# DIFF's sub-norm root by bits, exp and Newton steps on GpSimd; later transposes; compressed transposes in the other PSUM bank

## Chip, cores, metric

One core of a Trainium2 chip. The metric is the device time of one launch in microseconds. The engines are TensorE (PE; its weight loads are PEld), VectorE (DVE), ScalarE (ACT), GpSimd (POOL) and SyncE (SP), which issues all DMAs here. Each runs its own instructions in program order; they meet at semaphores.

## The reference, cut to what matters

The program is one layer of a decoder on 512 tokens of width 1024 in fp32: a combined projection, three token mixers (NSA: compressed, selected and window attention; DIFF: differential attention; FOX: forgetting attention), gates that merge them, an output product and a convolutional feed-forward part. The change lies in DIFF's sub-norm and in the start of NSA's compressed attention. The sub-norm:

```
ob = diff_attention(qb, kb, dv.reshape(B, S, DIFF_HEADS, 2 * hd), lam)
o_b = (rms_norm(ob, diff_subln_g[l]) * (1.0 - lam_init)).reshape(B, S, BRANCH_WIDTH)
# rms_norm(x, g) = x * rsqrt(mean(x * x) + EPS) * g, over the 128 values of each head
```

So each of the 512 tokens and 4 heads needs one value (mean + EPS) ** -0.5: four columns of 128 rows for each block of 128 tokens.

## The kernel before, in words

Every fp32 product is made of fp32r pieces: a weight block comes by DMA into `raw`, ScalarE rounds it to `wh`, VectorE subtracts to get `wl`, and TensorE runs three passes (L1277 to L1279). There are three attention stages in a row: NSA, DIFF, FOX. Each is laid out as a list of events in slots by `attention_events` (`put(j, ...)`), and all engines walk the same list, each doing its part of every event and waiting on semaphores for the others.

In DIFF there are 32 score units (4 query blocks of 8: 4 heads by 2 maps); the keys grow from 128 to 512 with the block. The events of a slot come in this order: S (TensorE's scores L1425 to L1428 in one of two banks; VectorE's maximum L1048; ScalarE's Exp L737, which frees the bank), C (VectorE's combination of two maps, L1053 to L1058, at every even slot), G (about five of the 192 gate products, L1455; after every 24th ScalarE takes a Tanh, L753), A (transposes of the combined probabilities, L1305, copied by VectorE L1067 or ScalarE L743), O (values, L1441; copied by VectorE into `otok`, L1077), SUB, SUN, OT, WL (VectorE's weight piece, L850), W (ScalarE's, L585). A unit's values come five slots behind its scores, so the last of block i falls in slot 8(i + 1) - 1 + 5, called `last`: 12, 20, 28, 36.

The sub-norm of block i: SUB at `last`: ScalarE squares `otok` (L768) and loads the table set that has Ln and Exp (L769), VectorE sums per head into `hss` (L1108). SUN one slot later: ScalarE takes Ln (L594) and Exp with scale -0.5 (L595) in `inv_rms`, VectorE multiplies `otok` by the result (L1112). OT three slots after `last` (the last block: between the two halves P of FOX's query projection): TensorE transposes `otok` (L1305), ScalarE rounds with the gain into `oT_h` (L777), VectorE takes the rest into `oT_l` (L1116). `otok` has two buffers, by the block's parity.

Behind the last slot the list goes on with the weight pieces W and WL of the projection's second half, then P 0, OT, P 1; then `post` takes the norms of FOX's queries, again with `inv_rms`. GpSimd copies keys before DIFF's slots (L1247, L1248), and merges branch results after them (L1255); between these it has no work.

In NSA's head the order is written out by hand (`first`): gate products G, and SC (compressed scores), CN (their softmax), T (transposes of window keys), TC (transposes of the compressed probabilities, copied by ScalarE to `pcT`, L762), OC (their values). SC, TC and OC use the bank that the running gate chunk of 24 products does not use: `spare = 1 - f // GATE_STEPS % 2`.

Of the kernel before, what the change touches and what calls it, by code (L numbers as in the profile page):

```python
# [19 lines left out]

P = 128
S = 512
# [2 lines left out]
TT = S // P  # L25
# [82 lines left out]
def attention_events(m):  # L108

    U = len(units_of(m))
    per = U // TT
    t_lag, o_lag = (3, 5) if m == DIFF else (2, 3)
    at = {}  # L120

    def put(j, *event):
        at.setdefault(j, []).append(event)

    tail = 20 if m == FOX else 0
    head = HEAD_FILL[m]
    slots = U + o_lag
    for piece in range(4):
        if m > NSA:
            put(piece, "W", BI[(m, "gate1")], piece)  # L130
            put(piece + 1, "WL", BI[(m, "gate1")], piece)

    def put_fill(j, f0, f1):
        put(j, "G", f0, f1)
        for f in range(f0, f1):
            if (f + 1) % (2 * GATE_STEPS) == 0:
                b = BI[(m, "gate0")] + f // (2 * GATE_STEPS) + 2
                for piece in range(4):

                    if m < FOX or b < BI[(m, "gate3")] + 2:  # L140
                        put(j + 1 + piece, "W", b, piece)
                        put(j + 2 + piece, "WL", b, piece)

    if m == NSA:

        head = 40
        for i in range(1, TT):
            put(per * i - 12, "SC", i)
            put(per * i - 10, "CN", i)
            put(per * i - 8, "TC", i)  # L150
            put(per * i - 6, "OC", i)
    for j in range(slots):
        n = FILL - tail - head
        put_fill(j, head + n * j // slots, head + n * (j + 1) // slots)
        if j < U:
            put(j, "S", j)
    for q in range(U):
        if has_pv(m, q):
            put(q + 1, "C", q)
            put(q + t_lag, "A", q)  # L160
            put(q + o_lag, "O", q)
    for i in range(TT):
        last = per * (i + 1) - 1 + o_lag
        if m == DIFF:
            put(last, "SUB", i)
            put(last + 1, "SUN", i)
            if i < TT - 1:
                put(last + 3, "OT", i)
        elif i < TT - 1:
            put(last + 1, "OT", i)  # L170
    order = {k: n for n, k in enumerate(("S", "C", "CN", "TC", "OC", "G", "SC", "A", "O", "SUB", "SUN", "OT", "WL", "W"))}
    out = [e for j in sorted(at) for e in sorted(at[j], key=lambda e: order[e[0]])]
    first = [("G", 0, HEAD_FILL[m])]
    if m == NSA:
        b = BI[(m, "gate1")]
        first = [("G", 0, 8), ("SC", 0), ("W", b, 0), ("G", 8, 16), ("CN", 0), ("WL", b, 0), ("W", b, 1), ("G", 16, 24), ("T", 0), ("WL", b, 1),
                 ("W", b, 2), ("TC", 0), ("G", 24, 32), ("T", 1), ("WL", b, 2), ("W", b, 3), ("OC", 0), ("WL", b, 3), ("G", 32, head)]
    if m == FOX:
        out += [("G", FILL - tail, FILL - 8), ("OT", TT - 1), ("G", FILL - 8, FILL), ("W", BI[(m, "gate3")] + 2, None), ("WL", BI[(m, "gate3")] + 2, None)]
    else:  # L180
        out += [("P", 0), ("OT", TT - 1), ("P", 1)]
    return first + out


def build(nc, x, wblk, w1, w2, params, consts, out):
# [85 lines left out]
    with ExitStack() as ctx:  # L271
# [113 lines left out]
        neglam = small("neglam", [P, 1])  # L385
        valid = small("valid", [P, 1])
        kss = small("kss", [HD, 1])
        assert base + used[0] <= nc.sbuf_usable_end, (base + used[0], nc.sbuf_usable_end)

        ps = [ctx.enter_context(nc.psum_tensor(f"ps{i}", [P, S], f32)) for i in range(8)]  # L390

        def sem(name):
            return ctx.enter_context(nc.semaphore(name))
# [29 lines left out]
        const_ready = sem("const_ready")  # L423
        k_zero = sem("k_zero")
        k_twice = sem("k_twice")
        cpe_ready = sem("cpe_ready")
        ksq_ready, kss_ready = sem("ksq_ready"), sem("kss_ready")
        sub_sq = sem("sub_sq")
# [68 lines left out]
        NORMS = [n for m, n in NORM_JOBS]  # L497

        rs_order = [("N", 0), ("nq", 0), ("nq", 1), ("KC",)] + [(n, r) for n in ("sw", "dq", "dk") for r in range(2)]
        rs_order += [("SUB", i) for i in range(TT)] + [(n, r) for n in ("fq", "fk") for r in range(2)] + [("N", 1)]  # L500
        rs_at = {k: n + TT for n, k in enumerate(rs_order)}

        def operands(m, u):
# [62 lines left out]
        def _(act):  # L566
# [128 lines left out]
            for m in (NSA, DIFF, FOX):  # L695
# [33 lines left out]
                for e in EVENTS[m]:  # L729
                    what, j = e[0], e[1] if len(e) > 1 else None  # L730
                    if what == "T":
                        post_t(m, PROJ[m][-1], (2 * j, 2 * j + 1))
                    if what == "S":
                        s0, n = span(units[j])
                        b = place[("S", m, j)][0]
                        act.wait_ge(max_ready, unit_no(m, j) + 1)
                        nc.scalar.activation(prob[:, j % 4, 0:n], ps[b][:, 0:n], ACT.Exp, bias=nmx[:, j:j + 1],  # L737
                                             accum_out=lsum[:, j:j + 1]).then_inc(psum_free[b], 1)
                    elif what == "A" and pv_index(m, j) % 2 == 1:
                        s0, n = span(units[j])  # L740
                        b = place[("A", m, j)][0]
                        full(act, ("A", m, j))
                        nc.scalar.activation(probT[:, 1, 0:n], ps[b][:, 0:n], ACT.Copy).then_inc(psum_free[b], 1)  # L743
                    elif what == "G":
                        for f in range(e[1], e[2]):
                            if (f + 1) % GATE_STEPS == 0:
                                c = f // GATE_STEPS
                                full(act, ("G", m, c))
                                if m > NSA:
                                    free(act, ("B", m - 1, c))  # L750
                                b = place[("G", m, c)][0]

                                nc.scalar.activation(gate[:, c, :], ps[b][:, :], ACT.Tanh, scale=0.5).then_inc(psum_free[b], 1)  # L753
                    elif what == "W":
                        split(j, e[2])
                    elif what == "SC":
                        free(act, ("SC", j))
                        nc.scalar.activation(pc[:, j % 2], pc[:, j % 2], ACT.Exp).then_inc(cexp_ready, 1)
                    elif what == "TC":
                        b = place[("TC", j)][0]  # L760
                        full(act, ("TC", j))
                        nc.scalar.activation(pcT[:, :, :], ps[b][:, 0:256].rearrange("p (e t) -> p e t", e=2),  # L762
                                             ACT.Copy).then_inc(psum_free[b], 1)
                    elif what == "SUB":
                        last = len(units) // TT * (j + 1) - 1
                        free(act, ("O", m, last - 2))
                        free(act, ("O", m, last))
                        nc.scalar.activation(sq[:, 0, :], otok[:, j % 2, :], ACT.Square).then_inc(sub_sq, 1)  # L768
                        nc.scalar.preload_act_table_set(LN_EXP)  # L769
                    elif what == "SUN":  # L770
                        act.wait_ge(sub_sums, j + 1)
                        inv_rms(rstd[:, 4 * j:4 * j + 4], hss[:, j, 0:4], P)
                    elif what == "OT":
                        b = place[("OT", m, j)][0]
                        full(act, ("OT", m, j))

                        nc.scalar.activation(oT_h[:, :, j * P:(j + 1) * P], ps[b][:, :].rearrange("p (k t) -> p k t", k=4), ACT.Copy,  # L777
                                             scale=par[:, C_SUBLN:C_SUBLN + 1] if m == DIFF else 1.0).then_inc(oT_hi, 1)
# [56 lines left out]
        def _(dve):  # L835
# [174 lines left out]
            for m in (NSA, DIFF, FOX):  # L1010
# [28 lines left out]
                for e in EVENTS[m]:  # L1039
# [67 lines left out]
                        dve.wait_ge(sub_sq, j + 1)  # L1107
                        nc.vector.tensor_reduce(hss[:, j, 0:4], sq[:, 0, :].rearrange("p (h c) -> p h c", c=P), AX.X, ALU.add).then_inc(sub_sums, 1)  # L1108
                    elif what == "SUN":
                        dve.wait_ge(rstd_ready, rs_at[("SUB", j)])  # L1110
                        v = otok[:, j % 2, :].rearrange("p (h c) -> p h c", c=P)
                        nc.vector.tensor_tensor(v, v, rstd[:, 4 * j:4 * j + 4].unsqueeze(2).to_broadcast([P, 4, P]), ALU.mult).then_inc(sub_ready, 1)  # L1112
                    elif what == "OT":
                        dve.wait_ge(oT_hi, TT * m + j + 1)
                        b = place[("OT", m, j)][0]
# [102 lines left out]
        @block.gpsimd  # L1218
        def _(pool):

            pool.wait_ge(const_in, 32)
            full(pool, ("N", 0, KD - 1))
            nc.gpsimd.tensor_copy(valid[:, :], stage[:, K_VALID:K_VALID + 1])
# [19 lines left out]
            for m in (DIFF, FOX):  # L1243
                for c in range(4):

                    pool.wait_ge(hi_taken, hi_at[("T", m, PROJ[m][1], c)])
                    nc.gpsimd.tensor_copy(k_hh[64:128, 2 * c, :], k_hh[0:64, 2 * c, :])  # L1247
                    nc.gpsimd.tensor_copy(k_hh[0:64, 2 * c + 1, :], k_hh[64:128, 2 * c + 1, :]).then_inc(k_twice, 1)  # L1248
                for c in range(KD):

                    free(pool, ("B", m, c))
# [475 lines left out]
```

## Time and profile before

| | us |
|---|---|
| median of 3 runs | 1028.97 |
| lowest, highest | 1026.33, 1029.14 |
| profiled execution, its time | 1028.74 |
| profiled execution, its span | 1027.0 |
| busy PE, DVE, ACT, POOL | 1004.2, 561.5, 402.1, 95.9 |

The profile is of one execution. Its span leaves out 1.7 us that the time has around it. Times in rows count from the span's start. DIFF's slots run from about 324 to 411 us; the NSA head from about 88 to 104 us. TensorE counts as busy while a product runs, also at half clock, so its busy time alone does not tell whether it runs at full speed; the granted clock (1.00 for 2.4 GHz, 0.50 for 1.2 GHz, a mean over a window) does.

### The profile page before, as it was taken

The page shows a single profiled execution, that of the slowest core. Times are in us where ns is not written, and L with a number is a line of the kernel's source. Part 1 is how long each engine was busy: PE and PEld are TensorE (multiplying, and loading weights), DVE is VectorE, ACT ScalarE, POOL GpSimd, SP SyncE. Part 2 cuts the span into 40 slices and gives each one's busy share as a digit, 9 for nine tenths or more (in the row PEclk, how much of TensorE's full clock was granted, in tenths as well). Part 3 has the DMA queues.
Part 4 walks back from the last instruction along what each step waited for, and adds up shares of the span by engine and source line. Part 5 has one row for each costly group of instructions (what it writes and reads, how often), then busy time and mean ns, then how long its engine had stood idle before and what let it go on. Part 6 is the DMA issues. An engine that isn't in the chain of part 4 may idle for free.

```text
span 1027.0 us, 13047 instructions
## 1 busy us (share of the span) xinstructions
PE 1004.2 (98%) x5101; PEld 844.2 (82%) x5101; DVE 561.5 (55%) x1035; ACT 402.1 (39%) x729; POOL 95.9 (9%) x84
## 2 busy tenths in 40 slices
PE   6999999999999899999999999999999999999998
PEld 5777889998888677888888888888888888888887
DVE  5746887763565576456555445465655565621213
ACT  5335454534346655424644334342322323212110
POOL 3200000010002000030200031012121112200000
PEclk9999999999999899999999999999999999999999
DMA  6521110102322111232211125222322322322322
GB/s 246 208 80 44 42 43 1 42 1 93 113 82 82 41 42 41 97 109 83 83 42 42 41 82 200 87 82 83 117 89 82 123 82 86 119 82 94 112 83 82
DMA packets 13693, 86.91 MB, mean 85 GB/s; under 512 B 1472, under 2 KB 1984, under 8 KB 4160
## 3 DMA queue, kind: packets, MB, share of 16 engines
q1 hardware_dynamic: 13632, 86.07, 23.7%
q8 instruction: 42, 0.69, 0.3%
q14 instruction: 19, 0.16, 0.1%
HBM read 83.96 MB, written 2.10 MB: 84 GB/s over the span
## 4 chain that ended last, share of the span: by engine, by line
PE 93%; DVE 3%; ACT 3%; issue 1%; DMA 0%; SPq 0%; ACTq 0%; DVEq 0%
PE ps L1277 21%; PE ps L1279 21%; PE ps L1278 21%; PE ps L1455 11%; PE ps L1441 5%; PE ps L1305 4%; PE ps L1427 2%; PE ps L1428 2%; PE ps L1425 1%; PE ps L1332 1%; DVE wl L850 1%; PE ps L1418 1%; PE ps L1358 1%; ACT prob L737 0%; DMA x<-x 0%
## 5 line engine op out<-in xcount | busy, mean ns | idle before, releaser
L850 DVE TENSOR_TENSOR wl<-raw,wh 128x512 fp32r<-128x512 f32 (+2 forms) x118 | 171.7, 1459 | 128.0 <-ACT wh L582 126.6
L582 ACT ACTIVATE wh<-raw 128x2048 fp32r<-128x2048 f32 (+1 forms) x58 | 109.4, 1886 | 152.5 <-PE ps L1279 141.3
L1277 PE MATMUL ps<-aT_h,wh 128*128 128x512 f32 (+1 forms) x376 | 146.8, 390 | 0.9 <-DVE aT_l L859 0.9
L1278 PE MATMUL ps<-aT_l,wh 128*128 128x512 f32 (+1 forms) x376 | 146.4, 389 | 0.0
L1279 PE MATMUL ps<-aT_h,wl 128*128 128x512 f32 (+1 forms) x376 | 146.4, 389 | 0.0
L737 ACT ACTIVATE prob<-ps,nmx 128x384 f32<-128x384 f32 (+3 forms) x128 | 66.6, 520 | 120.5 <-DVE nmx L1048 120.3
L1277 PE MATMUL ps<-wh,aT_h 128*128 128x512 f32 x256 | 102.2, 399 | 0.0
L1279 PE MATMUL ps<-wh,aT_l 128*128 128x512 f32 x256 | 100.1, 391 | 0.0
L1278 PE MATMUL ps<-wl,aT_h 128*128 128x512 f32 x256 | 99.8, 390 | 0.0
L1277 PEld LDWEIGHTS ps<-aT_h,wh 128*128 128x128 f32 (+1 forms) x376 | 70.0, 186 | 16.6 <-issue 1.1
L1279 PEld LDWEIGHTS ps<-aT_h,wl 128*128 128x128 f32 (+1 forms) x376 | 70.0, 186 | 15.4
L1278 PEld LDWEIGHTS ps<-aT_l,wh 128*128 128x128 f32 (+1 forms) x376 | 70.0, 186 | 15.0
L1455 PE MATMUL ps<-aT_h,wh 128*128 128x512 f32 x192 | 76.8, 400 | 1.6 <-ACT pcT L762 1.6
L1455 PE MATMUL ps<-aT_l,wh 128*128 128x512 f32 x192 | 77.8, 405 | 0.0
L1455 PE MATMUL ps<-aT_h,wl 128*128 128x512 f32 x192 | 77.5, 403 | 0.0
L1441 PE MATMUL ps<-V,probT 128*128 128x64 f32 (+1 forms) x544 | 75.9, 270 | 1.0 <-DVE probT L1067 0.8
L1048 DVE TENSOR_REDUCE nmx<-ps 128x1 f32<-128x384 f32 (+3 forms) x128 | 61.3, 479 | 28.0 <-PE ps L1428 26.9
L1441 PEld LDWEIGHTS ps<-V,probT 128*128 128x128 f32 x544 | 71.0, 195 | 5.2 <-DVE probT L1067 2.5
L1277 PE MATMUL ps<-wh,actT_h 128*128 128x512 f32 x176 | 68.5, 389 | 0.0
L1279 PE MATMUL ps<-wh,actT_l 128*128 128x512 f32 x176 | 68.5, 389 | 0.0
L1278 PE MATMUL ps<-wl,actT_h 128*128 128x512 f32 x176 | 68.5, 389 | 0.0
L1260 POOL TENSOR_TENSOR gl<-gl,rstdT 128x512 f32<-128x512 f32 x22 | 44.5, 2022 | 234.6 <-ACT gl L824 234.6
(209 smaller groups left out, 1720.6 us busy)
## 6 DMA issues: line engine op xcount, KB each, us to landing
raw<-wblk SPq DMA_DIRECT2D x72, 1024.0 KB, 4.7
x<-x SPq DMA_DIRECT2D x4, 512.0 KB, 5.2
w_sb<-w SPq DMA_DIRECT2D x1, 2048.0 KB, 9.2
hid<-x SPq DMA_DIRECT2D x1, 2048.0 KB, 7.5
out<-outt SPq DMA_DIRECT2D x8, 256.0 KB, 2.0
stage<-consts SPq DMA_DIRECT2D x1, 1216.5 KB, 11.5
later<-consts SPq DMA_DIRECT2D x1, 448.0 KB, 12.2
par<-params SPq DMA_DIRECT2D x1, 204.5 KB, 8.6
```

Of the source, the lines that this page charges most:

```text
L582: nc.scalar.activation(wh[b % 2][:, 0:n], raw[b % RING][:, 0:n], ACT.Copy).then_inc(hi_ready, 4)
L737: nc.scalar.activation(prob[:, j % 4, 0:n], ps[b][:, 0:n], ACT.Exp, bias=nmx[:, j:j + 1], accum_out=lsum[:, j:j + 1]).then_inc(psum_free[b ...
L850: ins = nc.vector.tensor_tensor(wl[b % RING][:, cols], raw[b % RING][:, cols], wh[b % 2][:, cols].bitcast(f32), ALU.subtract)
L1048: nc.vector.tensor_reduce(nmx[:, j:j + 1], bank(("S", m, j))[:, 0:n], AX.X, ALU.max, negate=True).then_inc(max_ready, 1)
L1260: nc.gpsimd.tensor_tensor(gl[:, c, :], gl[:, c, :], rstdT[:, :], ALU.mult).then_inc(glr_ready, 1)
L1277: nc.tensor.matmul(dst, a_h, b_h, start=start, stop=False)
L1278: nc.tensor.matmul(dst, a_h, b_l, start=False, stop=False)
L1279: return nc.tensor.matmul(dst, a_l, b_h, start=False, stop=stop)
L1305: ins = nc.tensor.transpose(bk[:, n * P:(n + 1) * P], src, ident[:, :])
L1427: nc.tensor.matmul(dst, q_hl[:, qh, t], k_hh[:, kh, s0:s0 + n], start=False, stop=False)
L1441: ins = nc.tensor.matmul(bk[:, 0:vw], probT[:, pv_index(m, q) % 2, kb * P:(kb + 1) * P], V[:, s0 // P + kb, v0:v0 + vw], start=kb == 0, st ...
L1455: ins = nc.tensor.matmul(bk[:, :], (l if p == 2 else h)[:, k, cols], (aT_l if p == 1 else aT_h)[:, k], start=f % GATE_STEPS == 0, stop=f % ...
```

## The change

- SUB loads no table. SUN moves from `last` + 1 to `last` + 5 (17, 25, 33; the last block stays at 37), and OT from `last` + 3 to `last` + 7 (19, 27, 35).
- The inverse root no longer uses Ln. When VectorE's sums are there, GpSimd computes the mean plus EPS (`smean`) and subtracts 127 * 2 ** 23 from its bits read as an integer (`slog`, about the binary logarithm in steps of 2 ** -23). In SUN, ScalarE takes one Exp of it (`sy`, a guess at the inverse root). GpSimd then makes three Newton steps of four 128x4 instructions each, every one waiting for the one before by the semaphore `pool_link`; the last releases VectorE's multiplication by `sub_rstd`.
- The DIFF norms leave the list of `rstd_ready` results (`rs_order`).
- In the NSA head four gate products come before TC instead of behind it. They begin chunk 1, so `spare` for TC is bank 0 instead of bank 1; SC stays in bank 1, OC in bank 0.

```diff
--- before.py
+++ after.py
@@ -17,6 +17,7 @@
 import concourse.bass as bass
 from concourse import mybir
 from contextlib import ExitStack
+import math
 
 P = 128
 S = 512
@@ -163,9 +164,9 @@
         last = per * (i + 1) - 1 + o_lag
         if m == DIFF:
             put(last, "SUB", i)
-            put(last + 1, "SUN", i)
+            put(last + (5 if i < TT - 1 else 1), "SUN", i)
             if i < TT - 1:
-                put(last + 3, "OT", i)
+                put(last + 7, "OT", i)
         elif i < TT - 1:
             put(last + 1, "OT", i)
     order = {k: n for n, k in enumerate(("S", "C", "CN", "TC", "OC", "G", "SC", "A", "O", "SUB", "SUN", "OT", "WL", "W"))}
@@ -174,7 +175,7 @@
     if m == NSA:
         b = BI[(m, "gate1")]
         first = [("G", 0, 8), ("SC", 0), ("W", b, 0), ("G", 8, 16), ("CN", 0), ("WL", b, 0), ("W", b, 1), ("G", 16, 24), ("T", 0), ("WL", b, 1),
-                 ("W", b, 2), ("TC", 0), ("G", 24, 32), ("T", 1), ("WL", b, 2), ("W", b, 3), ("OC", 0), ("WL", b, 3), ("G", 32, head)]
+                 ("W", b, 2), ("G", 24, 28), ("TC", 0), ("G", 28, 32), ("T", 1), ("WL", b, 2), ("W", b, 3), ("OC", 0), ("WL", b, 3), ("G", 32, head)]
     if m == FOX:
         out += [("G", FILL - tail, FILL - 8), ("OT", TT - 1), ("G", FILL - 8, FILL), ("W", BI[(m, "gate3")] + 2, None), ("WL", BI[(m, "gate3")] + 2, None)]
     else:
@@ -385,6 +386,7 @@
         neglam = small("neglam", [P, 1])
         valid = small("valid", [P, 1])
         kss = small("kss", [HD, 1])
+        smean, slog, sy, st = (small(n, [P, 4]) for n in ("smean", "slog", "sy", "st"))
         assert base + used[0] <= nc.sbuf_usable_end, (base + used[0], nc.sbuf_usable_end)
 
         ps = [ctx.enter_context(nc.psum_tensor(f"ps{i}", [P, S], f32)) for i in range(8)]
@@ -423,6 +425,7 @@
         const_ready = sem("const_ready")
         k_zero = sem("k_zero")
         k_twice = sem("k_twice")
+        mean_ready, guess_ready, sub_rstd, pool_link = (sem(n) for n in ("mean_ready", "guess_ready", "sub_rstd", "pool_link"))
         cpe_ready = sem("cpe_ready")
         ksq_ready, kss_ready = sem("ksq_ready"), sem("kss_ready")
         sub_sq = sem("sub_sq")
@@ -497,7 +500,7 @@
         NORMS = [n for m, n in NORM_JOBS]
 
         rs_order = [("N", 0), ("nq", 0), ("nq", 1), ("KC",)] + [(n, r) for n in ("sw", "dq", "dk") for r in range(2)]
-        rs_order += [("SUB", i) for i in range(TT)] + [(n, r) for n in ("fq", "fk") for r in range(2)] + [("N", 1)]
+        rs_order += [(n, r) for n in ("fq", "fk") for r in range(2)] + [("N", 1)]
         rs_at = {k: n + TT for n, k in enumerate(rs_order)}
 
         def operands(m, u):
@@ -766,10 +769,10 @@
                         free(act, ("O", m, last - 2))
                         free(act, ("O", m, last))
                         nc.scalar.activation(sq[:, 0, :], otok[:, j % 2, :], ACT.Square).then_inc(sub_sq, 1)
-                        nc.scalar.preload_act_table_set(LN_EXP)
                     elif what == "SUN":
-                        act.wait_ge(sub_sums, j + 1)
-                        inv_rms(rstd[:, 4 * j:4 * j + 4], hss[:, j, 0:4], P)
+
+                        act.wait_ge(mean_ready, j + 1)
+                        nc.scalar.activation(sy[:, :], slog[:, :], ACT.Exp, scale=-0.5 * math.log(2.0) / 2 ** 23).then_inc(guess_ready, 1)
                     elif what == "OT":
                         b = place[("OT", m, j)][0]
                         full(act, ("OT", m, j))
@@ -1107,9 +1110,9 @@
                         dve.wait_ge(sub_sq, j + 1)
                         nc.vector.tensor_reduce(hss[:, j, 0:4], sq[:, 0, :].rearrange("p (h c) -> p h c", c=P), AX.X, ALU.add).then_inc(sub_sums, 1)
                     elif what == "SUN":
-                        dve.wait_ge(rstd_ready, rs_at[("SUB", j)])
+                        dve.wait_ge(sub_rstd, j + 1)
                         v = otok[:, j % 2, :].rearrange("p (h c) -> p h c", c=P)
-                        nc.vector.tensor_tensor(v, v, rstd[:, 4 * j:4 * j + 4].unsqueeze(2).to_broadcast([P, 4, P]), ALU.mult).then_inc(sub_ready, 1)
+                        nc.vector.tensor_tensor(v, v, sy[:, :].unsqueeze(2).to_broadcast([P, 4, P]), ALU.mult).then_inc(sub_ready, 1)
                     elif what == "OT":
                         dve.wait_ge(oT_hi, TT * m + j + 1)
                         b = place[("OT", m, j)][0]
@@ -1218,6 +1221,7 @@
         @block.gpsimd
         def _(pool):
 
+            plinks = [0]
             pool.wait_ge(const_in, 32)
             full(pool, ("N", 0, KD - 1))
             nc.gpsimd.tensor_copy(valid[:, :], stage[:, K_VALID:K_VALID + 1])
@@ -1246,6 +1250,27 @@
                     pool.wait_ge(hi_taken, hi_at[("T", m, PROJ[m][1], c)])
                     nc.gpsimd.tensor_copy(k_hh[64:128, 2 * c, :], k_hh[0:64, 2 * c, :])
                     nc.gpsimd.tensor_copy(k_hh[0:64, 2 * c + 1, :], k_hh[64:128, 2 * c + 1, :]).then_inc(k_twice, 1)
+                for i in range(TT if m == DIFF else 0):
+
+                    def plink(ins):
+                        plinks[0] += 1
+                        ins.then_inc(pool_link, 1)
+                        pool.wait_ge(pool_link, plinks[0])
+
+                    pool.wait_ge(sub_sums, i + 1)
+                    if i > 0:
+                        pool.wait_ge(sub_ready, i)
+                    plink(nc.gpsimd.tensor_scalar(smean[:, :], hss[:, i, 0:4], 1.0 / P, EPS, ALU.mult, ALU.add))
+                    nc.gpsimd.tensor_scalar(slog[:, :], smean[:, :].bitcast(mybir.dt.int32), 127.0 * 2 ** 23, None, ALU.subtract).then_inc(mean_ready, 1)
+                    pool.wait_ge(guess_ready, i + 1)
+                    for step in range(3):
+                        plink(nc.gpsimd.tensor_tensor(st[:, :], sy[:, :], sy[:, :], ALU.mult))
+                        plink(nc.gpsimd.tensor_tensor(st[:, :], st[:, :], smean[:, :], ALU.mult))
+                        plink(nc.gpsimd.tensor_scalar(st[:, :], st[:, :], -0.5, 1.5, ALU.mult, ALU.add))
+                        ins = nc.gpsimd.tensor_tensor(sy[:, :], sy[:, :], st[:, :], ALU.mult)
+                        if step < 2:
+                            plink(ins)
+                    ins.then_inc(sub_rstd, 1)
                 for c in range(KD):
 
                     free(pool, ("B", m, c))
```

## Rows read from the trace of the kernel before

**Rows 1.** The page, the chain that ended last, by engine.

```profile
PE 93%; DVE 3%; ACT 3%; issue 1%; DMA 0%; SPq 0%; ACTq 0%; DVEq 0%
```

**Rows 2.** TensorE's waits: line, releaser, total us, times, longest us.

```profile
PE ps L1305 <- DVE otok L1112: 4.0, 1, 4.0
...
PE ps L1425 <- ACT prob L737: 2.2, 3, 1.3
...
PE ps L1305 <- DVE prob L1058: 2.0, 1, 2.0
...
PE ps L1455 <- ACT pcT L762: 1.6, 1, 1.6
```

**Rows 3.** Windows: length; busy us (count) of PE, PEld, DVE, ACT, POOL; granted clock; DMA.

```profile
350.00:355.00 5.00, 1.11 (x5) 0.56 (x3) 0.64 (x2) 4.26 (x6) 0.00 (x0) 0.90 0.00 0
...
355.00:358.50 3.50, 2.97 (x9) 2.48 (x10) 2.64 (x9) 1.56 (x6) 0.00 (x0) 0.50 0.00 0
...
358.50:362.00 3.50, 3.50 (x15) 2.93 (x15) 2.94 (x9) 1.10 (x3) 0.00 (x0) 0.66 0.00 0
...
381.00:383.00 2.00, 0.83 (x4) 0.35 (x2) 1.92 (x6) 0.74 (x2) 0.00 (x0) 1.00 0.00 0
...
405.00:409.00 4.00, 3.94 (x17) 3.67 (x18) 1.69 (x5) 0.60 (x1) 0.00 (x0) 0.57 0.00 0
```

**Rows 4.** Timeline of the first sub-norm: start, us, engine, line, operation [idle before <-releaser].

```profile
349.31 1.28 ACT L753 ACT_TABLE_LOAD   x1
...
351.22 1.28 ACT L594 ACT_TABLE_LOAD   x1
...
352.83 1.28 ACT L595 ACT_TABLE_LOAD   x1
...
354.36 0.69 DVE L1112 TENSOR_TENSOR otok<-otok,rstd 128x512 f32<-128x512 f32 x1 [5.81 <-ACT rstd L595]
```

**Rows 5.** Groups by form: the preloads of SUB (count, busy us, mean ns).

```profile
L769 ACT ACT_TABLE_LOAD x4 | 5.1, 1283 | 0.1
```

**Rows 6.** Timeline, a table load in a norm at the end of NSA.

```profile
251.29 1.28 ACT L595 ACT_TABLE_LOAD   x1
```

**Rows 7.** Groups by form on GpSimd (count, busy us, mean ns, idle before).

```profile
L1224 POOL CAST identr<-stage 128x128 fp32r<-128x128 f32 x1 | 0.3, 289 | 0.0
...
L1225 POOL CAST distD<-stage 128x512 fp32r<-128x512 f32 x1 | 0.6, 609 | 0.0
...
L1230 POOL TENSOR_SCALAR biasC<-stage 128x128 fp32r<-128x128 f32 x8 | 4.1, 527 | 0.3
...
L1223 POOL COPY valid<-stage 128x1 f32<-128x1 f32 x1 | 0.6, 587 | 16.9 <-DMA later<-consts 16.9
```

**Rows 8.** Timeline, slots 17 and 20 of DIFF, and the Exp of a later norm.

```profile
360.94 0.42 PE L1425 MATMUL ps<-distD,slopeI 128*128 128x384 f32 x1
...
361.85 0.55 DVE L1048 TENSOR_REDUCE nmx<-ps 128x1 f32<-128x384 f32 x1
...
362.44 0.58 ACT L737 ACTIVATE prob<-ps,nmx 128x384 f32<-128x384 f32 x1 [1.56 <-DVE nmx L1048]
...
366.76 0.33 PE L1425 MATMUL ps<-distD,slopeI 128*128 128x384 f32 x1
...
373.59 0.20 ACT L595 ACTIVATE rstd<-lnv 128x4 f32<-128x4 f32 x1
```

**Rows 9.** Groups by form on VectorE: a tiny instruction.

```profile
L1054 DVE TENSOR_SCALAR coef<-rl,neglam 128x1 f32<-128x1 f32 x16 | 3.4, 214 | 0.6
```

**Rows 10.** Timeline, the last sub-norm, the weight pieces, the projection's second half.

```profile
414.56 0.69 DVE L1112 TENSOR_TENSOR otok<-otok,rstd 128x512 f32<-128x512 f32 x1 [1.16 <-ACT rstd L595]
...
415.17 2.50 DVE L850 TENSOR_TENSOR wl<-raw,wh 128x512 fp32r<-128x512 f32 x4
...
422.72 0.48 PE L1277 MATMUL ps<-wh,aT_h 128*128 128x512 f32 x1
```

**Rows 11.** Timeline, chunk 1's first gate product in the NSA head.

```profile
98.27 0.47 PE L1455 MATMUL ps<-aT_h,wh 128*128 128x512 f32 x1 [1.63 <-ACT pcT L762]
```

## The prediction

> **What bounds the kernel now.** I read the page first: of the chain that ended last, 93% is TensorE [rows 1]. So only what makes TensorE idle or slow can be won. The list of waits on TensorE is short [rows 2]: 4.0 us for the sub-norm's result (`otok`, L1112), 2.2 us in three waits for the score exponentials, 2.0 us for the combined probabilities (`prob`, L1058), and 1.6 us for the compressed transposes' copy (`pcT`). The granted clock adds what waits do not show [rows 3]. In 350 to 355 us its mean is 0.90, which is 1.0 us at half clock; 355 to 358.5 is all half; 358.5 to 362 at 0.66 is 2.4 us more. So the clock is at 1.2 GHz instead of 2.4 GHz for about 6.9 us, from about 354.0 to 360.9; TensorE stood idle before it fell, and resumed at 355.1, so 5.8 us of work ran at half speed and cost half of that, 2.9 us. After the 2.0 us wait, 405 to 409 at 0.57 is 3.4 us at half, 1.7 us lost. The DIFF stage thus loses 4.0 + 2.9 + 2.2 + 2.0 + 1.7 = 12.8 us, the NSA head 1.6 us.
>
> The timeline tells why [rows 4]. After the first head tile ScalarE goes through three table loads: one for the gate's Tanh, then one each for Ln and Exp, 1.28 us each. VectorE sits in its queue at the multiplication L1112 for 5.81 us, and TensorE reaches the transposes two slots later and waits 4.00 us. The 2.0 us at 405 us is indirect: VectorE was late with the combination L1058, having waited for the sub-norm of slot 29 and for `oT_h` of slot 31.
>
> **The change, part by part.**
>
> 1. *Table loads.* The four preloads at L769 go [rows 5]; with them the two inside the first norm and the three that bring Tanh's set back inside DIFF: nine loads. Exp has run in Tanh's set all along, so the new guess needs none. Against that the projection of FOX's queries no longer finds the Ln set: Ln, Exp, Ln, Exp then load one table each, as the same code does at the end of NSA, where both norms show it [rows 6] (one of the four loads). 4 x 1.28 = 5.1 us on ScalarE, under weight products of TensorE; at the end of NSA no TensorE wait stands there. I cost these at nothing. If that cover failed, they would cost up to 5.1 us.
>
> The row shows 1.28 us per load with ScalarE's next instruction 0.01 to 0.03 us behind it (352.83 + 1.28 against the result at 354.36 [rows 4]). The Trainium skill, ScalarE: Activation LUTs, "What ACT_TABLE_LOAD costs", gives the same 1283 ns but adds a drain of about 1380 ns to each switch; nine loads less would then free 24 us of ScalarE rather than 11.5. These rows leave no room for the drain, and neither figure enters my sum.
>
> 2. *The first sub-norm's stall* goes as it stands: nothing in slot 13 waits any more. Saved 4.0 + 2.9 = 6.9 us. The waits around the second and third norm (2.2, 2.0 with 1.7) are saved too, since slots 21 to 24 and 29 to 31 lose their old norms; what comes in their place is term 3.
>
> 3. *The new chain.* ScalarE issues the guess only in slot 17, 25, 33 (last + 5), and VectorE stands at L1112 in the same slot. Between them lie 12 dependent GpSimd instructions of 128x4, each with a semaphore. The mean and the integer subtraction run in the four free slots and cost nothing. So VectorE's queue is blocked for guess plus 12 links, and behind it stand the next maximum, the combination and the weight split; ScalarE's exponentials wait for the maxima and TensorE's scores for those.
>    One link: no row shows a GpSimd instruction of 4 elements. The nearest [rows 7]: a cast of 128x128 takes 289 ns and of 128x512 609 ns, 0.83 ns per element, so four elements would be 0.19 us; a TENSOR_SCALAR of 128x128 takes 527 ns, less 124 elements 0.42 us; a copy of 128x1, the first of its kind, 587 ns. I take the middle of the first two, 0.30, plus 0.05 for the semaphore (the exponential starts 0.04 us behind the maximum that it waits for [rows 8]): 0.35, T = 12 x 0.35 = 4.2 us. Ends: 0.19 gives 2.3 us, 0.587 gives 7.0 us.
>    The rule against it stands in the Trainium skill, GPSIMD Engine Reference, "Engine selection": elementwise work belongs on VectorE, GpSimd is about twice as slow. Twice VectorE's own tiny instruction (214 ns for 128x1 [rows 9]) would make T 5.1 us plus 0.6 for the semaphores, and each stall below 1.5 us longer; no row of before shows GpSimd at this size.
>    The stall, counted from the start of the score product of slot 17 (360.94) [rows 8]: its maximum runs from +0.9 to +1.45, the exponential to +2.1 and its accumulator read to +2.25, the guess 0.2 (as L595 [rows 8]) to +2.5, the chain to 2.5 + T, the multiplication 0.69 [rows 4] to 3.2 + T. Then the maximum of slot 18 (0.55) and its exponential (0.6) free the bank at 4.4 + T. TensorE wants that bank at +5.8 (366.76 less 360.94) plus 0.45 for the four transposes, 6.25. So it loses about T - 1.8 = 2.4 us, most of it at the transposes. A 2.0 us wait drew 1.7 us of lost clock, and the one of 1.3 us at 381 to 383 us none [rows 2, 3], so I add 1.7: 4.1 us. The same in slot 25 (512 keys, the slots a little longer, taken as equal): 8.2 us. The third falls in slot 33, where no scores are left, the guess no longer waits for a fresh maximum, and TensorE has two slots of gate products: nothing.
>    Before slot 34 VectorE has six slots without a norm to catch up, hence no second 2.0 us wait.
>
> 4. *The last sub-norm* (slot 37) has 11 us of projection behind it, but the weight pieces stand behind it on VectorE. They end now at 415.17 + 2.50 = 417.7 and are wanted at 422.72 [rows 10]. The mean (0.7), guess (0.2) and T replace a wait of 1.16 us [rows 10]: later by T - 0.25 = 4.0 us, inside the 5.0 us of slack. Nothing, up to T = 5.3.
>
> 5. *GpSimd's and SP's queues.* 56 tiny instructions stand before the merges L1255, which come only behind the branch products of the stage's end: nothing. No DMA is added or moved; weights are released earlier as TensorE is.
>
> 6. *Compressed transposes.* Four gate products begin chunk 1 before TC, so TC takes the other bank, whose Tanh is long done, and the chunk no longer waits for `pcT`: 1.6 us saved [rows 11]. Four more gate products then cover the copy before OC.
>
> Sum: -12.8 + 8.2 - 1.6 = -6.2 us. The profiled execution took 1028.74 us (span 1027.0), 0.2 under the median 1028.97, so 1022.5 in its terms and **1022.8 us** against the median.
>
> **Rivals.**
> - *Cheap links* (T about 2.5 us): losses T - 1.8 = 0.7 us twice, no half clock: -12.8 + 1.4 - 1.6 = -13.0, 1016 us. For it: the cast's slope. Against: TENSOR_SCALAR's row. 0.15.
> - *The late combination stays* [rows 2, 3]: the norms in slot 25 hold VectorE up as those in 29 did, and TensorE still waits 2.0 us at slot 34 with 1.7 us of half clock: 1026.5 us. For it: the new stall in slot 25 is longer than the old one. Against: six slots to recover. 0.15.
> - *Dear links, slower than before*: 0.587 us each, T = 7.0: the stall of slots 17 and 25 is 5.2 us each with 2.9 us of half clock, 16.2, and the weights of the projection come 1.7 us late: -12.8 + 16.2 + 1.7 - 1.6 = +3.5, 1032.5 us. It decides from T = 6.1 (0.51 us a link), where 2 x (4.3 + 2.9) eats all 14.4. The only row of so small an operand is this price; against it, it is a first call. 0.12.
> - *It does not do what it says*: the guess brings its own table load, so each norm again costs loads: with 1.28 us in each of two stalls, and a reload for Tanh, about 1026. Against: Exp runs in Tanh's set now. 0.04.
>
> **Numbers.** The forecast (links of 0.28 to 0.43 us, T 3.3 to 5.1) spans 1019 to 1025.5 and has 0.54. The range 1017 to 1030 takes in the first three. A measurement of this kernel can tell about 0.3% (3.1 us) from no change. Faster by more: nearly all of the forecast, cheap links and a third of the late combination, 0.70; within: 0.19; slower: dear links, 0.11.
>
> **What would show it.** VectorE's wait at L1112 twice about 5 us, released by GpSimd, then short; links near 0.35 us; TensorE waits of 2 to 3 us at the transposes or scores of slots 19 and 20, 27 and 28, with half clock; none at 351 and 405; five table loads fewer; no wait at `pcT`. A per-link time above 0.5 us or below 0.25 us, or a wait before the projection's second half, would make the prediction wrong.

## The result, and the profile after

Five runs of each gave a median of 1022.09 us (1021.33 to 1022.57) for the changed kernel and 1027.15 us (1026.33 to 1029.14) for the kernel before: ratio 0.9945, 95% interval 0.9930 to 0.9959. A second comparison gave 1022.45 against 1028.71 us, ratio 0.9940 (0.9926 to 0.9954). So the change saves 5 to 6 us; 6.2 were forecast.

The profiled execution took 1021.33 us, its span 1019.5. The chain that ended last, by engine, is still TensorE's [rows 1]:

```profile
PE 93%; DVE 4%; issue 1%; POOL 1%; DMA 1%; ACT 1%; SPq 0%; DVEq 0%; ACTq 0%
```

TensorE's waits (line, releaser, total us, times, longest us) are others than [rows 2]. The 4.0, 2.0 and 1.6 us are gone, the waits for score exponentials have grown from 2.2 to 4.8 us, and three short ones stand at the transposes:

```profile
PE ps L1450 <- ACT prob L740: 4.8, 6, 1.7
...
PE ps L1330 <- DVE otok L1115: 1.8, 3, 1.0
```

The same columns as [rows 3], first where the old stall stood, then at three places with a new wait: the granted clock is 1.00 throughout. No single wait in this stage exceeds 1.7 us, and the half clock of [rows 3] did not return.

```profile
350.00:355.00 5.00, 5.00 (x32) 4.51 (x31) 1.77 (x5) 0.95 (x5) 1.61 (x9) 1.00 0.16 25
...
355.00:358.50 3.50, 2.63 (x14) 1.83 (x13) 2.35 (x6) 1.26 (x4) 0.76 (x4) 1.00 0.63 267
...
378.00:382.00 4.00, 2.83 (x14) 1.88 (x13) 3.50 (x8) 1.16 (x3) 0.27 (x2) 1.00 0.71 238
...
400.00:404.00 4.00, 2.97 (x20) 2.64 (x20) 1.65 (x3) 1.28 (x2) 0.25 (x2) 1.00 0.00 0
```

The new chain in slot 17, against [rows 4, 8]: TensorE's scores, VectorE's maximum, ScalarE's exponential and guess, the first and the last of GpSimd's twelve, VectorE's multiplication, the transposes, the scores of slot 20.

```profile
350.47 0.42 PE L1450 MATMUL ps<-distD,slopeI 128*128 128x384 f32 x1
...
351.29 0.56 DVE L1051 TENSOR_REDUCE nmx<-ps 128x1 f32<-128x384 f32 x1
...
351.88 0.58 ACT L740 ACTIVATE prob<-ps,nmx 128x384 f32<-128x384 f32 x1 [1.69 <-DVE nmx L1051]
...
352.45 0.20 ACT L775 ACTIVATE sy<-slog 128x4 f32<-128x4 f32 x1
...
352.73 0.20 POOL L1267 TENSOR_TENSOR st<-sy 128x4 f32<-128x4 f32 x1 [6.78 <-ACT sy L775]
...
355.81 0.20 POOL L1270 TENSOR_TENSOR sy<-sy,st 128x4 f32<-128x4 f32 x1
...
356.04 0.69 DVE L1115 TENSOR_TENSOR otok<-otok,sy 128x512 f32<-128x512 f32 x1 [4.19 <-POOL sy L1270]
...
356.79 0.66 PE L1330 MATMUL ps<-ident,otok 128*128 128x128 f32 x4 [0.36 <-DVE otok L1115]
...
357.96 0.44 PE L1450 MATMUL ps<-distD,slopeI 128*128 128x384 f32 x1 [0.51 <-ACT prob L740]
```

VectorE stands still for the 4.19 us up to the multiplication at 356.04, nearly all of it while the guess (352.45) and GpSimd's chain run; TensorE waits 0.36 us at the transposes and 0.51 us for the exponential behind it. In the slots of the first three norms VectorE waits at that line three times, and once more, 4.21 us, at the last norm (slot 37):

```profile
DVE otok L1115 <- POOL sy L1270: 10.8, 3, 4.3
```

GpSimd's twelve instructions by line, over four norms (count, busy us, mean ns | idle before), where [rows 7] had only larger ones:

```profile
L1267 POOL TENSOR_TENSOR st<-sy 128x4 f32<-128x4 f32 x12 | 2.8, 234 | 22.7 <-ACT sy L775 22.1
...
L1268 POOL TENSOR_TENSOR st<-st,smean 128x4 f32<-128x4 f32 x12 | 2.4, 199 | 0.9
...
L1269 POOL TENSOR_SCALAR st<-st 128x4 f32<-128x4 f32 x12 | 2.3, 193 | 1.0
...
L1270 POOL TENSOR_TENSOR sy<-sy,st 128x4 f32<-128x4 f32 x12 | 2.9, 246 | 1.0
```

In slot 17 the twelve start at 352.73 and the last ends at 356.01: 3.28 us, 0.28 us a link, about 0.20 of it busy and 0.08 between.

Lengths of stretches show where the time went. "Head" is from the first product of the compressed scores to the first score product of NSA, "NSA's slots" from there to DIFF's first score product, "DIFF" from that to the first product of FOX's query projection.

| kernel | head, us | NSA's slots, us | DIFF, us |
|---|---|---|---|
| before | 13.96 | 220.59 | 87.04 |
| after | 12.11 | 220.59 | 82.07 |
| after, second profile | 12.11 | 220.59 | 82.07 |

The head gave 1.85 us, DIFF 4.97 us, together 6.8. The profiled execution of before lay 1.6 us above the median of its five and that of the changed kernel 0.8 us under its own, hence 7.4 us between the profiles and about 5 between the medians.

### The profile page after: what moved, and what is told of

The parts are those of the page before. It is cut to its first block, busy times and chain, and to the rows that moved or that the text cites. A ratio compares the mean times of both kernels' runs of the same rounds, so it can differ in the third digit from the quotient of the medians.

```text
span 1019.5 us, 13097 instructions
## 1 busy us (share of the span) xinstructions
PE 999.9 (98%) x5101; PEld 840.3 (82%) x5101; DVE 561.7 (55%) x1035; ACT 394.0 (39%) x720; POOL 108.5 (11%) x140
## 4 chain that ended last, share of the span: by engine, by line
PE 93%; DVE 4%; issue 1%; POOL 1%; DMA 1%; ACT 1%; SPq 0%; DVEq 0%; ACTq 0%
PE ps L1302 22%; PE ps L1304 22%; PE ps L1303 22%; PE ps L1480 11%; PE ps L1466 5%; PE ps L1330 4%; PE ps L1452 2%; PE ps L1453 2%; PE ps L1450 1%; DVE nmx L1051 1%; DMA par<-params 1%; PE ps L1357 1%; PE ps L1443 1%; DVE wl L853 1%; DVE prob L1061 0%
## 5 line engine op out<-in xcount | busy, mean ns | idle before, releaser
L853 DVE TENSOR_TENSOR wl<-raw,wh 128x512 fp32r<-128x512 f32 (+2 forms) x118 | 172.2, 1464 | 127.8 <-ACT wh L585 126.5
```

What stands on the lines that cost most here:

```text
L853: ins = nc.vector.tensor_tensor(wl[b % RING][:, cols], raw[b % RING][:, cols], wh[b % 2][:, cols].bitcast(f32), ALU.subtract)
```

## Experiments

Each was timed beside the kernel before on the same chip, in five rounds; three chips were used.

**The head alone**, on the kernel before:

```diff
-                 ("W", b, 2), ("TC", 0), ("G", 24, 32), ("T", 1), ("WL", b, 2), ("W", b, 3), ("OC", 0), ("WL", b, 3), ("G", 32, head)]
+                 ("W", b, 2), ("G", 24, 28), ("TC", 0), ("G", 28, 32), ("T", 1), ("WL", b, 2), ("W", b, 3), ("OC", 0), ("WL", b, 3), ("G", 32, head)]
```

> The kernel before with only the NSA head's new order (four gate products ahead of TC). Theory (the 1.6 us wait for pcT goes and nothing takes its place): 1.6 to 1.9 us less than before, 1025.2 to 1025.6; the wait at the gate product for pcT is gone and the stage DIFF looks as before, with its 4 us wait and the half clock. Rival (the whole 2.6 us by which the two profiles differ at the first score product of NSA come from this edit): 1024.5.

Measured: ratio 0.9985 (0.9974 to 0.9996), 1027.70 against 1028.96 us: 1.3 to 1.5 us, a little under the 1.6 to 1.9 expected. The head took 12.10 us, so the rival falls: 0.8 of the 2.6 us between the profiles arose before the head. But DIFF took 88.13 us, 1.1 more than before with the same instructions. Its waits are those of [rows 2], but for 2.6 us instead of 2.2 at the score exponentials. Most of the difference is in place by slot 18, and the windows of this run show where it comes from:

```profile
349.50:354.50 5.00, 0.90 (x6) 0.42 (x4) 1.52 (x3) 3.38 (x5) 0.00 (x0) 1.00 0.00 0
...
354.50:358.00 3.50, 2.74 (x7) 2.47 (x8) 2.19 (x8) 1.98 (x6) 0.00 (x0) 0.51 0.00 0
...
358.00:361.50 3.50, 3.50 (x13) 3.10 (x12) 2.94 (x9) 0.67 (x2) 0.00 (x0) 0.51 0.00 0
```

TensorE resumed at 353.7 us, and all 6.8 us of half clock lay behind that, where in [rows 3] it had begun 1.1 us ahead of TensorE's return: about 0.5 us more lost, and a wait of 0.88 instead of 0.42 us behind the transposes. The cost of a half clock depends on how it falls, which differs between executions.

**The slots alone**, on the kernel before (Ln and Exp kept):

```diff
-            put(last + 1, "SUN", i)
+            put(last + (5 if i < TT - 1 else 1), "SUN", i)
             if i < TT - 1:
-                put(last + 3, "OT", i)
+                put(last + 7, "OT", i)
```

> The kernel before with SUN and OT moved to last + 5 and last + 7, the root still by Ln and Exp on ScalarE, with its preload in SUB. A Tanh now lies between every preload and its norm, so each of the three norms should bring two loads, a chain of about 3.1 us in place of GpSimd's 3.5. Theory A (what counts is that the norm falls in longer slots, and VectorE's wait stays under about 4.5 us): VectorE waits about 4 us three times, no half clock, 1022.5 to 1024.5. Theory B (what counts is that ScalarE is rid of the loads): 1026 to 1028.

Measured: 0.9972 (0.9961 to 0.9982), 1026.05 against 1028.96 us: 2.9 us saved, against the 4.5 to 6.5 of theory A; by its time the run lies at the edge of theory B's range. DIFF took 84.49 us. TensorE's waits in DIFF, and a window in the columns of [rows 3]:

```profile
PE ps L1425 <- ACT prob L737: 4.6, 6, 1.7
...
PE ps L1305 <- DVE otok L1112: 2.7, 2, 1.4
...
384.00:388.00 4.00, 3.41 (x8) 2.70 (x9) 2.08 (x5) 2.73 (x7) 0.00 (x0) 0.57 0.36 150
```

The waits look like those of the changed kernel, but for 0.9 us more at the transposes, and one piece of half clock came back: 3.4 us of it, so 1.7 us lost, behind waits of 1.30 and 0.75 us. Each theory has a part: the later slots alone are worth 2.5 of the 5.0 us that DIFF gained, and the new root on top of them the other 2.4.

**The root alone**: the changed kernel with SUN and OT back in their old slots:

```diff
-            put(last + (5 if i < TT - 1 else 1), "SUN", i)
+            put(last + 1, "SUN", i)
             if i < TT - 1:
-                put(last + 7, "OT", i)
+                put(last + 3, "OT", i)
```

> The kernel after with SUN and OT back at last + 1 and last + 3, the root by GpSimd. Theory A (as in the run with the slots alone): the first norm's slots are short (256 keys), so the transposes still wait 1.5 to 3 us for it, with some half clock, and the second and third now wait for 12 links instead of two ScalarE instructions: 1024 to 1026. Theory B (the loads were the cost): 1022 to 1022.8.

Measured: 1.0030 (1.0020 to 1.0041), 1032.39 against 1028.96 us: with the head's gain in it, it is slower than the kernel before, and over 6 us above theory A's range. DIFF took 90.33 us in the profiled execution, which with 1029.87 us was the shortest of eleven. TensorE's waits there:

```profile
PE ps L1330 <- DVE otok L1115: 6.2, 3, 2.9
...
PE ps L1330 <- DVE prob L1061: 3.0, 2, 2.0
...
PE ps L1450 <- ACT prob L740: 2.9, 3, 1.1
```

All nine table loads are gone, and yet the stage is 3.3 us longer: theory B falls. The first wait shrank from 4.0 to 2.9 us, but the second and third norms wait for 12 links in place of two ScalarE instructions. In the old slots GpSimd's root costs 3.3 us, in the later ones it gains 2.4.

**The guess early**, on the changed kernel: a new event GUE in slot `last + 2` (within a slot it comes behind SUB) takes over ScalarE's part of SUN; VectorE's multiplication stays at `last + 5`.

```diff
+            put(last + (2 if i < TT - 1 else 1), "GUE", i)
             put(last + (5 if i < TT - 1 else 1), "SUN", i)
...
-                    elif what == "SUN":
+                    elif what == "GUE":
                         act.wait_ge(mean_ready, j + 1)
```

> The kernel after with ScalarE's guess in slot last + 2 (a new event), the multiplication left at last + 5. The chain of 12 links (3.3 us) then runs under three slots. Theory: VectorE's waits at the multiplication (4.19, 4.29, 2.32 us) fall under 0.3 us, TensorE's waits in DIFF from 6.6 us to 1 to 2.5 us, 1018 to 1020. Rival (VectorE itself is the bound of the 384- and 512-key slots, and the wait turns up at the scores): 1021 to 1022.

Measured: 0.9856 (0.9843 to 0.9870), 1013.89 us; and in a later comparison:

> The early guess once more, as the measure for the runs beside it: 14 to 15 us under the kernel before.

0.9860 (0.9845 to 0.9874), 1013.62 us. It beats both kernels: 15 us under the kernel before, about 8.5 us under the changed one, where 2 to 4 were expected. TensorE's waits in its whole span are these, with none of over 0.5 us in DIFF (L1451 is its score product; the 8.0 us stand at the program's start, and in the kernel before too, with 7.9):

```profile
PE ps L1384 <- DVE xn L993: 8.0, 1, 8.0
...
PE ps L1303 <- DVE aT_l L863: 0.9, 1, 0.9
...
PE ps L1467 <- DVE probT L1071: 0.8, 1, 0.8
...
PE ps L1451 <- ACT prob L741: 0.5, 1, 0.5
```

Guess, last link and multiplication of the first norm:

```profile
348.07 0.21 ACT L776 ACTIVATE sy<-slog 128x4 f32<-128x4 f32 x1
...
351.86 0.20 POOL L1271 TENSOR_TENSOR sy<-sy,st 128x4 f32<-128x4 f32 x1
...
352.21 0.68 DVE L1116 TENSOR_TENSOR otok<-otok,sy 128x512 f32<-128x512 f32 x1
```

The chain took 3.7 us here, with VectorE busy beside it, and VectorE never waits for it in these three norms. DIFF took 74.05 us. I take that as the stage without its losses, as TensorE is busy for 73.55 of it: before lost 87.04 - 74.05 = 13.0 us, the changed kernel still 8.0.

**A longer and a shorter chain**, on the changed kernel (six steps change nothing but time; two, with `range(2)` and `step < 1`, leave the root less exact):

```diff
-                    for step in range(3):
+                    for step in range(6):
...
-                        if step < 2:
+                        if step < 5:
```

> The kernel after with six Newton steps instead of three: 24 links of 0.28 us, T = 6.7 us instead of 3.3. Theory (the chain stands in VectorE's queue, which has almost no slack): VectorE's three waits grow by 3.3 us each, TensorE loses at least 3 x 3.3 = 10 us more, and as its single waits now pass 2 us the half clock returns, up to 3 us at each: 10 to 19 us over the kernel after. Rival (part of the wait is slack of the two slots up to the transposes): under 6 us over it.

Measured: 1035.15 us beside 1022.45 of the changed kernel, ratio to before 1.0065 (1.0052 to 1.0078): 12.7 us more, as in the theory. TensorE's waits in DIFF, 11.3 us at the transposes alone (3.7, 3.8 and 3.9), with a stretch of 6.8 us of half clock at each:

```profile
PE ps L1330 <- DVE otok L1115: 11.3, 3, 3.9
...
PE ps L1450 <- ACT prob L740: 0.7, 1, 0.7
```

> The kernel after with two Newton steps: 8 links, T = 2.2 us. Theory (each link of the chain costs TensorE nearly its own length at three norms): 2 to 3.3 us under the kernel after. Rival (what is left of the waits comes from the order of the slots, not from the chain): within 1 us of it.

Measured: 1018.74 us, ratio 0.9906 (0.9892 to 0.9920), 3.7 us less; DIFF 78.75 us, 3.3 less. Four links less at three norms are 3 x 4 x 0.28 = 3.4 us, and slot by slot each of the three norms gives back 1.1 us: between these two lengths each microsecond of chain costs TensorE one microsecond. The rival falls. The changed kernel itself was run beside them:

> The changed kernel itself once more, as the measure for the runs beside it: 5 to 6 us under the kernel before.

**ScalarE's root early**, no GpSimd. The edit is to the kernel before; GUE, SUN and OT stand in the slots of the early guess, and the head has its new order:

```diff
-                        nc.scalar.preload_act_table_set(LN_EXP)
-                    elif what == "SUN":
+                    elif what == "GUE":
+                        nc.scalar.preload_act_table_set(LN_EXP)
                         act.wait_ge(sub_sums, j + 1)
```

> No GpSimd: the kernel before with the NSA head's new order, Ln and Exp on ScalarE in slot last + 2 with the table preload right ahead of them, the multiplication in last + 5 and the transposes in last + 7, as in the run with the early guess. Theory A (only the distance between the root and VectorE's multiplication counts): VectorE's waits there under 0.3 us, 1014 to 1016. Theory B (the loads and Ln on ScalarE hold up the score exponentials, which TensorE waits for): 1017 to 1021.

Measured: 1016.25 us, ratio 0.9881 (0.9865 to 0.9896); DIFF 76.28 us. That is just above theory A's range and below B's. Theory A in the main: of the 8.0 us by which the early guess shortens the changed kernel's DIFF, 5.8 come without GpSimd. The other 2.2 arise at slots 30 and 31 and have a place in the rows below. After a norm with Ln, the next Tanh brings its set back (377.05), the rounding of `oT_h` comes that much later, and VectorE waits 3.34 us for it where it waited 1.91 us with the early guess; the maxima behind it are late, and TensorE waits for the exponentials of two score products. So here, with the root out of VectorE's way, the loads do cost.

```profile
377.05 1.28 ACT L754 ACT_TABLE_LOAD   x1
...
379.55 0.75 DVE L1117 SCALAR_TENSOR_TENSOR oT_l<-ps,par,oT_h 128x512 fp32r<-128x512 f32 x1 [3.34 <-ACT oT_h L778]
...
381.77 0.50 PE L1426 MATMUL ps<-distD,slopeI 128*128 128x512 f32 x1 [0.58 <-ACT prob L738]
...
386.24 0.50 PE L1426 MATMUL ps<-distD,slopeI 128*128 128x512 f32 x1 [1.01 <-ACT prob L738]
```

**The Newton steps on VectorE**, in the changed kernel's slots, in place of its wait (`link` makes each wait for the one before; GpSimd's twelve are gone):

```diff
-                        dve.wait_ge(sub_rstd, j + 1)
+                        dve.wait_ge(guess_ready, j + 1)
+                        for step in range(3):
+                            link(nc.vector.tensor_tensor(st[:, :], sy[:, :], sy[:, :], ALU.mult))
+                            link(nc.vector.tensor_tensor(st[:, :], st[:, :], smean[:, :], ALU.mult))
+                            link(nc.vector.tensor_scalar(st[:, :], st[:, :], -0.5, 1.5, ALU.mult, ALU.add))
+                            link(nc.vector.tensor_tensor(sy[:, :], sy[:, :], st[:, :], ALU.mult))
```

> The kernel after with the twelve Newton instructions on VectorE, in place of its wait in the same slots (mean and guess as they were). A tiny VectorE instruction takes about 0.15 to 0.21 us and 0.04 to its successor, so 12 take 2.4 to 3.0 us against GpSimd's 3.3. Theory (VectorE stands still in that chain anyway, so it may as well compute it): 0.5 to 2.5 us under the kernel after, 1020 to 1022. Rival (VectorE is the bound and its busy time counts fully): at or over the kernel after.

Measured: 1020.40 us, ratio 0.9924 (0.9911 to 0.9937), against 0.9940 and 0.9945 of the changed kernel: about 2 us less, as the theory has it. A VectorE link:

```profile
L1116 DVE TENSOR_TENSOR st<-st,smean 128x4 f32<-128x4 f32 x12 | 1.9, 162 | 0.4
```

162 ns and 0.04 to the next, 0.20 us a link against GpSimd's 0.28. The elementwise rule of the Trainium skill (GPSIMD Engine Reference, "Engine selection") points the right way here, with 1.4 in place of twice. Whether it still would with the guess early was not run: there GpSimd's chain costs TensorE nothing, and VectorE is busy for 76% of the stage.

**A preload for the norms behind each stage**, on the kernel with the early guess. The line runs after NSA and after DIFF, so it serves DIFF's query norms as well as FOX's:

```diff
                     split(BI[(m, "br0")])
+                    nc.scalar.preload_act_table_set(LN_EXP)
                     post(m + 1, PROJ[m + 1][0])
```

> The kernel with the early guess, with one preload of the table set that has Ln and Exp ahead of the norms of FOX's queries: three of the four loads (3.8 us of ScalarE) go. Theory (they lie under weight products of TensorE): no difference from the early guess alone beyond 1 us, 1013 to 1015. Rival (ScalarE's lateness there reaches the branch products or FOX's first scores): 2 to 4 us under it.

Measured: 1013.82 us, beside 1013.62 without it; ratios 0.9859 and 0.9860. Six loads are gone, three at each place (18 in the whole span became 12), and the time is the same: those loads are hidden.

## Why the prediction was right, point by point

- **What is lost before**: 12.8 us in DIFF from waits and clock; against the early guess it is 13.0. Right.
- **Table loads**: nine fewer, four more (23 in the span became 18), and the four cost nothing (last experiment). The guess brings none: the rival on that falls. Taking the nine away does not help by itself (the root alone); it is worth 2 us once the norm stands late (the last two microseconds of ScalarE's root early).
- **The first stall** is gone. The waits around the old second and third norms are gone as well.
- **One link** was set at 0.35 us and is 0.28; T = 3.3 instead of 4.2 us. TENSOR_SCALAR's larger row misled: the 128x4 TENSOR_SCALAR took 0.19 us, the value of the cast's slope. What that slope missed was the 0.08 us between links, against 0.05 assumed.
- **The stall of 8.2 us** was measured as 8.0, by other parts, so the closeness of -6.2 is luck. Set against the early guess slot by slot, the first norm costs 3.0 us, the second 3.8, the third 1.2. For T = 3.3 the step "T - 1.8" gives 1.5 us for the first norm up to slot 20, and 1.3 was measured; but VectorE then stays behind, and TensorE waits again at slots 22 and 23, and after the second norm at 30 and 31. I had left these follow-up waits out. Too much in the sum were 0.9 us of chain and 1.7 us of half clock at each of two norms, 5.2 us; left out were 3.8 us behind the first two norms and 1.2 us at the third, 5.0 us. Of the signs named, the waits of 2 to 3 us with half clock did not show: the longest was 1.7 us, at full clock.
- **The third norm** was costed at nothing and took 1.2 us. The guess came at 395.78 us, but its chain ran beside a busy VectorE until 400.3 and took 4.3 us; its two slow links are below, each with the VectorE instruction beside it.

```profile
395.89 0.75 DVE L1061 SCALAR_TENSOR_TENSOR prob<-prob,coef 128x512 f32<-128x512 f32 x1
...
396.06 0.63 POOL L1267 TENSOR_TENSOR st<-sy 128x4 f32<-128x4 f32 x1 [6.24 <-ACT sy L775]
...
397.34 0.76 POOL L1270 TENSOR_TENSOR sy<-sy,st 128x4 f32<-128x4 f32 x1
...
397.35 0.69 DVE L853 TENSOR_TENSOR wl<-raw,wh 128x512 fp32r<-128x512 f32 x1
```

- **The projection's weights**: as forecast, inside the slack. Multiplication, weight pieces and the transposes between the halves are below, as in [rows 10]; the pieces end at 413.1 us, 1.7 us ahead of the transposes and 2.0 ahead of the second half's first product (415.15).

```profile
410.03 0.69 DVE L1115 TENSOR_TENSOR otok<-otok,sy 128x512 f32<-128x512 f32 x1 [4.21 <-POOL sy L1270]
...
410.64 2.49 DVE L853 TENSOR_TENSOR wl<-raw,wh 128x512 fp32r<-128x512 f32 x4
...
414.80 0.60 PE L1330 MATMUL ps<-ident,otok 128*128 128x128 f32 x4
```

- **The head**: 1.6 forecast, 1.85 measured in the stretch. TC no longer holds the chunk's bank, and OC finds its copy done:

```profile
95.40 0.48 PE L1480 MATMUL ps<-aT_h,wh 128*128 128x512 f32 x1
...
96.41 0.38 PE L1330 MATMUL ps<-ident,pc 128*128 128x128 f32 x2
...
96.96 0.39 ACT L765 ACTIVATE pcT<-ps 128x256 f32<-128x256 f32 x1
...
101.14 0.22 PE L1450 MATMUL ps<-distD,slopeI 128*128 128x128 f32 x1
```

- **The rivals**: the late combination did not stay, links were neither dear nor cheap. The break-even of the dear ones was set at T = 6.1 us. At T = 3.3 the kernel was 6.3 us faster than before and at 6.7 it was 6.4 us slower; a line between the two crosses at about 5.0, since nothing of a longer chain is covered at any of three norms. The recorded range, 1017 to 1030, takes in the late combination but not the 1016 of the cheap links.

## What to carry to other kernels

When one engine's result is awaited by an in-order queue, the slot in which the chain begins matters more than the engine that computes it: issue the first step as soon as its input is there, and put only the consumer late. Moving producer and consumer together, as here, leaves VectorE's wait about as long (9.9 us over four norms before, 11.4 with the slots alone) and puts it where TensorE loses less by it. Before costing a wait by its slack, look whether the waiting engine can catch up afterwards; VectorE, busy for 68% of the changed kernel's DIFF, could not: TensorE waited for exponentials up to six slots after the multiplication.

## What the runs showed of the hardware

- GpSimd's 128x4 TENSOR_TENSOR and TENSOR_SCALAR take about 0.20 us with 0.08 us to a dependent one. Some took 0.26 to 0.76 us. In the profiles with GpSimd's root each of these lies beside a VectorE weight piece, combination or scaling (L853, L1061 and L1060 in the changed kernel), and ends 0.05 to 0.06 us behind it; beside a maximum or a copy, which VectorE reads from `ps`, none was slow. So an early start does not shield the chain from VectorE: with the early guess it took 3.7 to 4.7 us.
- The spread of the kernel before goes with the granted clock. Of its 43 timed runs on three chips, 13 had a mean clock of 0.997 or 0.998 and took 1026.1 to 1027.0 us; 30 had 0.993 or 0.995 and took 1028.0 to 1030.1. The changed kernel, at 0.999 to 1.000, spread over 1.5 us in all its runs.
- Half clock came without a wait of over 1 us before it, too. In the run with six steps, the NSA stage has 3.4 us of it near 110 us (columns as in [rows 3]), with TensorE busy all the time; the runs with ScalarE's early root and with the Newton steps on VectorE have the like, the other profiles not. Its cause is open. It cost nothing: NSA's slots took 220.57 to 220.62 us in these three as in the others, whose wait of 0.8 us for `probT` there is missing from them.

```profile
109.00:113.00 4.00, 4.00 (x17) 3.30 (x16) 3.76 (x17) 2.94 (x9) 0.00 (x0) 0.60 0.00 0
```
